# Second mixer's products taken from activations without the row's factor, which is applied at eviction

## The chip, the core and the metric

The kernel is one program on one core of a Trainium2 chip. Its engines run side by side and meet at semaphores: TensorE (PE in the profile; PEld is its weight load), VectorE (DVE), ScalarE (ACT), GpSimd (POOL), and the queues that issue DMAs (SP for most of them). The metric is the device time of one execution, in microseconds. The measured time of three executions before the change is 765.91 us (median; 765.34 to 765.93).

## What is computed

The reference runs two transformer blocks over 256 tokens of 1024 features. The first is a latent attention mixer with a mixture of experts. The second starts from the first one's normalised output, normalises again, and feeds a mixer with two halves: a gated half (strips `u` and `v_a` through GELU, layer norm, a mix over positions) and an attention half (`q`, `k`, `v` and one forget gate per head).

```python
def rms_norm(x, g):
    xf = x.astype(jnp.float32)
    y = xf * lax.rsqrt(jnp.mean(xf * xf, axis=-1, keepdims=True) + EPS)
    return (y * g.astype(jnp.float32)).astype(x.dtype)
...
    return rmsnorm(x, final_norm_g)
...
        h = rms_norm(x, norm_mix_g[l])
        z = h @ w_in[l]
        o = 0
        u_a = jax.nn.gelu(z[..., o:o + D_A], approximate=False); o += D_A
        v_a = jax.nn.gelu(z[..., o:o + D_A], approximate=False); o += D_A
...
        f_logit = z[..., o:o + N_HEADS_B] + f_bias[l].astype(z.dtype)
        out_a = spatial_gating(u_a, v_a, sg_ln_g[l], sg_w[l], sg_b[l])
        out_b = forgetting_attention(q_b, k_b, v_b, f_logit)
        x = x + jnp.concatenate([out_a, out_b], axis=-1) @ w_out[l]
```

The line `return rmsnorm(x, final_norm_g)` ends the first block; the lines behind it are the second. `q_b`, `k_b` and `v_b` are cut from `z` like the two strips. Both norms multiply a token's row by one number, so both together are a gain per feature (the product of the two gains) times one factor per token.

## The kernel before

Activations lie with features on the partitions: `xT` is 8 tiles of 128 features by 256 tokens, T is 256, KD is 8. Every float32 product that matters is split: a weight `w` is rounded to `w_hi`, its rest is `w_lo`, and the same is done to the activation (`h2_hi`, `h2_lo`); TensorE then adds three products, hi by hi, lo by hi, hi by lo. ScalarE makes the high parts (`chunk_to_hi`, one instruction for 128x1024 elements of weights), VectorE the low parts (`chunk_to_lo`). The second mixer's input weights come as five loads of 2 MB into `ring`, cut into chunks: chunks 0 to 3 are the strips `va`, 4 to 7 the strips `u`, 8 to 11 the tiles q0, k0, q1, k1, 12 to 15 `v`, 16 to 19 q2, k2, q3, k3. `w_hi` and `w_lo` have room for four chunks each, so chunk c waits until chunk c-4 has been read (`chunk2_free`).

Every engine has one queue, and its order is the order in which its part of the source is written; nothing is scheduled by a program. What a wait holds up is therefore everything that is written after it for that engine.

The stretch that the change touches begins when the last expert is done. VectorE adds the expert sum to `xT` (eight instructions, L2446). Then comes a chain: ScalarE squares the eight tiles (L981), TensorE sums them over features (L1539) and turns the sums to one number per token (L1543), VectorE, ScalarE and VectorE make reciprocal roots (L2454 to L2457; `rs` columns 2 and 3 hold the factor of both norms for the two halves of the tokens), TensorE spreads them over the partitions (L1551, banks 6 and 7), VectorE multiplies (`mix_norm`, L2462), ScalarE rounds (L988), VectorE takes the rest (`mix_low`). While TensorE has nothing to do it runs matmuls on zeros (`stay_awake`, L1251). Then it runs the strips of `va` (L1731 to L1739; for each k-tile it uses both token halves), `u` in two strips (L1221 to L1225), the eight matmuls of the forget gates (L1805, weights `wr`), tiles q0, k0, q1 (L1195), the running sums of the gates (L1777, L1771), their spreading (L1793), and k1.

`PROD2` names the products and which engine evicts them from PSUM: A for ScalarE, D for VectorE. `BANK2` gives each one its bank. From the gates hangs a chain of its own: `forget` and `forget_end` (VectorE, with exponential and logarithm on ScalarE between), row sums (PE L1777), their copy (DVE L2535), spreading, the copies `nck` (ACT L1001), eight additions of a mask on GpSimd (L719, L724), and only then the first row maximum of the attention (DVE L2225).

The attention runs 16 units (one head and one half of the queries each). For each, TensorE makes scores (L1346), VectorE adds gates and mask and takes the maximum (L2225, L2227), ScalarE the exponential (L880), VectorE the division by the sum (L2235), TensorE the transpose (L1355), ScalarE its copy (L888). Between them stand the products of `v`, q2, k2, q3, k3 and their chunks. After it come the output product, a norm, and the feed-forward part, in which TensorE runs without a gap from about 571 us to 747 us.

## Time and profile before

| | us |
|---|---|
| median of three executions | 765.91 |
| the profiled execution | 766.22 |
| its span, first to last instruction | 764.43 |
| PE busy in the span | 738.8 |
| DVE busy | 408.4 |
| ACT busy | 309.5 |
| POOL busy | 30.1 |

The profile is of one execution, which lies 0.31 us above the median. Rows of the timeline begin with the start in microseconds from the span's start, and then the busy time; a later row of an engine may begin before the busy time of an earlier one ends, since instructions overlap a little, so the pace of a row of instructions is taken from their starts. What stands in brackets is the time for which the engine was idle just before, and what ended that. One float32 matmul of 256 columns or less is recorded as two instructions.

### The profile page before, as it was taken

Reading aid. Unit: us, or ns where it says so; the run is one execution under the profiler, and the core shown is the slowest. Engines: PE = TensorE matmul, PEld = TensorE weight load, DVE = VectorE, ACT = ScalarE, POOL = GpSimd, SP = SyncE. Lnnn points to the kernel's source line nnn. Section 1 sums busy time; section 2 is a strip of 40 time slices with the busy share of each in tenths; the row PEclk is TensorE's granted clock in tenths of the full one; section 3 lists DMA queues with packets and bytes.
Section 4 is the critical chain, followed back from the end, with each engine's and each line's share of the span. In section 5 each row is a group of like instructions: output and inputs, shape, how many; then the busy total and the mean of one; then the engine's idle time right before and its main releaser. Section 6 shows DMA issues by size and latency. Waiting matters only on the chain.

```text
span 764.4 us, 11513 instructions
## 1 busy us (share of the span) xinstructions
PE 738.8 (97%) x4546; PEld 519.1 (68%) x4550; DVE 408.4 (53%) x735; ACT 309.5 (40%) x555; POOL 30.1 (4%) x42
## 2 busy tenths in 40 slices
PE   8999999999998999999999999999999999999997
PEld 3597786454696344443454346877889999999885
DVE  1594704568756122211221137877768888888443
ACT  3463202555725002001110136665656666666333
POOL 0000020033000000000000000030000000000000
PEclk9999999999999999999999999999999999999999
DMA  9973123889689899999999997305305455495101
GB/s 374 397 326 118 22 88 111 291 325 377 274 336 386 316 431 426 426 412 428 427 430 420 420 427 301 111 1 214 145 1 192 157 202 204 141 422 208 69 0 56
DMA packets 19675, 199.00 MB, mean 260 GB/s; under 512 B 2192, under 2 KB 2704, under 8 KB 4016
## 3 DMA queue, kind: packets, MB, share of 16 engines
q1 hardware_dynamic: 18720, 194.82, 63.6%
q0 software_dynamic: 624, 3.28, 1.1%
q8 instruction: 30, 0.49, 0.3%
q10 hardware_dynamic: 288, 0.30, 0.1%
q14 instruction: 13, 0.11, 0.0%
HBM read 197.34 MB, written 1.05 MB: 260 GB/s over the span
## 4 chain that ended last, share of the span: by engine, by line
PE 79%; DMA 9%; DVE 5%; ACT 4%; issue 1%; POOL 1%; SPq 0%; ACTq 0%; DVEq 0%; POOLq 0%
PE banks L1645 12%; PE banks L1959 8%; PE banks L1195 7%; PE banks L1682 6%; DMA ring<-in_w_up 5%; PE banks L1921 5%; PE banks L1919 5%; PE banks L1915 5%; PE banks L1406 2%; PE banks L1600 2%; DMA ring<-in_w_mod 2%; PE banks L1153 2%; PE banks L1443 2%; DVE w_lo L2008 2%; PE banks L1444 2%; PE banks L1445 2%
## 5 line engine op out<-in xcount | busy, mean ns | idle before, releaser
L2008 DVE TENSOR_TENSOR w_lo<-ring,w_hi 128x1024 fp32r<-128x1024 f32 (+1 forms) x122 | 145.8, 1203 | 75.9 <-ACT w_hi L1069 25.3
L1645 PE MATMUL banks<-ring,att 128*64 128x512 f32 x448 | 113.3, 593 | 2.7 <-DMA ring<-in_w_up 2.7
L1645 PEld LDWEIGHTS banks<-ring,att 128*64 128x64 f32 x448 | 39.4, 137 | 58.0 <-issue 49.9
L769 ACT ACTIVATE w_hi<-ring 128x1024 fp32r<-128x1024 f32 x50 | 52.1, 1056 | 37.8 <-PE banks L1195 22.9
L2403 DVE TENSOR_TENSOR front<-front,banks 128x512 f32<-128x512 f32 x8 | 5.5, 688 | 95.4 <-PE banks L1645 95.4
L1064 ACT ACTIVATE w_hi<-ring 128x1024 fp32r<-128x1024 f32 x44 | 46.1, 1055 | 15.9 <-PE banks L1921 8.1
L1915 PE MATMUL banks<-h_hi,w_hi 128*128 128x256 f32 x320 | 44.9, 283 | 0.0
L1919 PE MATMUL banks<-h_hi,w_lo 128*128 128x256 f32 x320 | 44.9, 283 | 0.0
L1921 PE MATMUL banks<-h_lo,w_hi 128*128 128x256 f32 x320 | 44.9, 283 | 0.0
L1915 PEld LDWEIGHTS banks<-h_hi,w_hi 128*128 128x128 f32 x320 | 41.3, 192 | 0.0
L1919 PEld LDWEIGHTS banks<-h_hi,w_lo 128*128 128x128 f32 x320 | 41.3, 192 | 0.0
L1921 PEld LDWEIGHTS banks<-h_lo,w_hi 128*128 128x128 f32 x320 | 41.3, 192 | 0.0
L2376 DVE SCALAR_TENSOR_TENSOR ysb_lo<-banks,slot_w,ysb_hi 128x512 fp32r<-128x512 f32 x16 | 12.0, 751 | 52.2 <-ACT ysb_hi L962 28.9
L962 ACT ACTIVATE ysb_hi<-banks,slot_w 128x512 fp32r<-128x512 f32 x8 | 5.5, 688 | 75.1 <-PE banks L1682 75.1
L1069 ACT ACTIVATE w_hi<-ring 128x1024 fp32r<-128x1024 f32 x22 | 23.2, 1060 | 26.9 <-PE banks L1959 25.9
L1682 PE MATMUL banks<-ring,front 128*64 128x512 f32 x128 | 29.2, 598 | 0.0
L1682 PE MATMUL banks<-big,front 128*64 128x512 f32 x64 | 28.3, 595 | 0.6 <-DVE front L2405 0.6
L2182 DVE TENSOR_REDUCE nmax<-banks 128x2 f32<-128x1024 f32 x16 | 19.6, 1224 | 12.2 <-PE banks L1406 11.9
L1959 PE MATMUL banks<-w_lo,hid_hi 128*128 128x512 f32 x88 | 25.6, 390 | 0.1
L1959 PE MATMUL banks<-w_hi,hid_hi 128*128 128x512 f32 x88 | 25.5, 389 | 0.0
L1959 PE MATMUL banks<-w_hi,hid_lo 128*128 128x512 f32 x88 | 25.5, 389 | 0.0
L858 ACT ACTIVATE osb<-banks 128x512 f32<-128x512 f32 x32 | 17.4, 600 | 19.7 <-PE banks L1415 19.7
(381 smaller groups left out, 1479.7 us busy)
## 6 DMA issues: line engine op xcount, KB each, us to landing
ring<-in_w_up SPq DMA_DIRECT2D x21, 2048.0 KB, 9.8
ring<-in_w_mod SPq DMA_DIRECT2D x11, 2048.0 KB, 9.2
ring<-in_w_down SPq DMA_DIRECT2D x9, 2048.0 KB, 12.8
ring<-in_w_in SPq DMA_DIRECT2D x8, 2048.0 KB, 18.6
ring<-in_w_gate SPq DMA_DIRECT2D x8, 2048.0 KB, 14.7
ring<-in_w_up SPq DMA_DIRECT2D x12, 1024.0 KB, 7.8
ring<-in_w_down SPq DMA_DIRECT2D x9, 1024.0 KB, 13.2
big<-in_w_down SPq DMA_DIRECT2D x8, 1024.0 KB, 14.2
```

Of the source, the lines that this page charges most:

```text
L769: nc.scalar.activation(chunk_part(w_hi, chunk, c), chunk_src(chunk, c), ACT.Copy).then_inc(chunk_hi[stage], 1)
L1064: nc.scalar.activation(granule(w_hi, j, half), up_half_of(j, half), ACT.Copy).then_inc(wide_hi, 1)
L1069: nc.scalar.activation(w_hi[:, d % 2, half, :], down_half_of(d, half), ACT.Copy).then_inc(wide_hi, 1)
L1195: last = nc.tensor.matmul(dst, chunk_part(part, chunk, c)[:, k, :], x[:, k, :], start=(part is w_hi and x is x_hi and k == 0), stop=(n == ...
L1645: last = nc.tensor.matmul(bank[2 + j][CAP * e:CAP * (e + 1), :], xs[:, k, at:at + CAP], gate_or_up(n + e, k, odd), start=(k == (4 if turne ...
L1682: last = nc.tensor.matmul(bank[2 + half][CAP * e:CAP * (e + 1), :], hidT[:, f, CAP * e:CAP * (e + 1)], w_e, start=(f == 0), stop=(f == 3))
L1915: nc.tensor.matmul(dst, granule(w_hi, j, g)[:, k, :], h2_hi[:, k, :], start=(k == 0), stop=False)
L1919: nc.tensor.matmul(dst, granule(w_lo, j, g)[:, k, :], h2_hi[:, k, :], start=False, stop=False)
L1921: last = nc.tensor.matmul(dst, granule(w_hi, j, g)[:, k, :], h2_lo[:, k, :], start=False, stop=(k == KD - 1))
L1959: return nc.tensor.matmul(ytok(q, half)[:, :], x[:, kt, q * P:(q + 1) * P], part[:, kt // 2 % 2, kt % 2, half * 512:(half + 1) * 512], sta ...
L2008: return V.tensor_tensor(dst, src, high.bitcast(F32), ALU.subtract)
L2182: V.tensor_reduce(nmax[:, u:u + 2], both[:, :, :], AX, ALU.max, negate=True).then_inc(A["maxed"], 1)
```

## The change

The mixer's products are taken from `xT` times the gain per feature (`g_both`), without the factor per token.

- ScalarE no longer waits for the norm to make `h2_hi`: `scaled_to_hi` multiplies a tile of `xT` by its gains and rounds. VectorE's `scaled_to_lo` gives the rest. Residual additions, weight chunks 0 to 3 and these steps are interleaved. The squares stand between them, and the table load for the square root behind the last of them.
- TensorE starts with `strips_of_va`. The sums of the norm stand behind these strips, then the gates' eight matmuls (from `xT` with weights `wr_x`, that VectorE has scaled by the gains), then the turn to one number per token, the first quarter of strip u0, the spreading, and the rest of u0. All `stay_awake` matmuls of this place are gone.
- The factor is applied at eviction: on ScalarE as the scale of the GELU and of `v` (one number per partition), on VectorE for q and k (`out_by_token`, one instruction with the factors spread in `by_token`) and for the gates in `forget`. So q0, k0, q1, k1, q2, k2, q3 and k3 are evicted by VectorE, where ScalarE did it.
- VectorE's order around `forget` is other: the last multiplication of the layer norm (`layer_norm_weight`) and chunk 10 now stand behind the first steps of the gates.

```diff
-PROD2 = ([("va", i, "A") for i in range(2)] + [("u", i, "A") for i in range(2)] + [("q", 0, "A"), ("f", 0, "D"),
-         ("k", 0, "A"), ("q", 1, "A"), ("rows", 0, "D"), ("cq", 0, "D")] + [("nck", i, "A") for i in range(4)] + [("k", 1, "A")]
-         + [("v", i, "A") for i in range(2)] + [(kind, i, "A") for i in range(2, 4) for kind in ("q", "k")])
+PROD2 = ([("va", i, "A") for i in range(2)] + [("u", i, "A") for i in range(2)] + [("q", 0, "D"), ("f", 0, "D"),
+         ("k", 0, "D"), ("q", 1, "D"), ("rows", 0, "D"), ("cq", 0, "D")] + [("nck", i, "A") for i in range(4)] + [("k", 1, "D")]
+         + [("v", i, "A") for i in range(2)] + [(kind, i, "D") for i in range(2, 4) for kind in ("q", "k")])
...
-        NORM_BANK = [7, 7, 0, 7]
+        NORM_BANK = [7, 7, 5, 7]
...
-            prefetch(ACT.Sqrt)
-            act.wait_ge(used, windows * 96)
-            for k in range(KD):
-                act.wait_ge(resid_m, k + 1)
-                nc.scalar.activation(sq[:, k, :], xT[:, k, :], ACT.Square).then_inc(squared, 1)
-            chunk_to_hi(1, CHUNK2, 0)
+            act.wait_ge(used, windows * 96)
+            def scaled_to_hi(ks):
+                for k in ks:
+                    act.wait_ge(resid_m, k + 1)
+                    nc.scalar.activation(h2_hi[:, k, :], xT[:, k, :], ACT.Identity, scale=g_both[:, k:k + 1]
+                                         ).then_inc(h2_hi_done, 1)
...
+            chunk_to_hi(1, CHUNK2, 0)
+            scaled_to_hi(range(4))
+            chunk_to_hi(1, CHUNK2, 1)
+            square(range(4))
+            chunk_to_hi(1, CHUNK2, 2)
+            scaled_to_hi(range(4, 6))
+            chunk_to_hi(1, CHUNK2, 3)
+            scaled_to_hi(range(6, KD))
+            square(range(4, KD))
+            prefetch(ACT.Sqrt)
             act.wait_ge(var, NORM_STEP[2] + 1)
             nc.scalar.activation(rs[:, 0:4], rs[:, 0:4], ACT.Sqrt).then_inc(std, 1)
...
-                    ins = nc.scalar.activation(vg[:, i, :], src[:, :], ACT.Gelu)
+                    ins = nc.scalar.activation(vg[:, i, :], src[:, :], ACT.Gelu, scale=rs[:, 2 + i:3 + i])
...
             prefetch(ACT.Gelu)
+            act.wait_ge(inv2, 1)
...
-            norm_sum(2, lambda: stay_awake(4, 2))
-            stay_awake(4, 2)
...
             strips_of_va()
-            product2("u", 0)
+            norm_sum(2, lambda: product2("u", 0, (0,)), gates_of_heads)
+            product2("u", 0, (1, 2, 3))
             product2("u", 1)
...
+            residual(range(4))
+            chunk_to_lo(1, CHUNK2, 0)
+            scaled_to_lo((0, 1))
+            chunk_to_lo(1, CHUNK2, 1)
+            scaled_to_lo((2, 3))
+            residual((4, 5))
+            chunk_to_lo(1, CHUNK2, 2)
+            scaled_to_lo((4, 5))
+            residual((6, 7))
+            chunk_to_lo(1, CHUNK2, 3)
+            scaled_to_lo((6, 7))
...
-            chunk_to_lo(1, CHUNK2, 0)
+            chunk_to_lo(1, CHUNK2, 4)
+            by_token = rstd[:, T:2 * T]
             dve.wait_ge(spread, 1)
+            link(V.tensor_copy(by_token, bank[6][:, 0:T]))
+            for c in range(5, 8):
+                chunk_to_lo(1, CHUNK2, c)
+            def out_by_token(kind, i):
+                n = at2(kind, i)
+                dve.wait_ge(prod2_ready, n + 1)
+                dst, scale = (q2, HD ** -0.5) if kind == "q" else (k2, 1.0)
+                V.scalar_tensor_tensor(dst[:, i, :], bank[BANK2[n]][:, 0:T], scale, by_token, ALU.mult, ALU.mult
+                                       ).then_inc(prod2_d, 1)
...
             layer_norm_end()
+            out_by_token("q", 0)
+            forget()
             chunk_to_lo(1, CHUNK2, 10)
-            forget()
+            layer_norm_weight()
+            forget_end()
+            out_by_token("k", 0)
             chunk_to_lo(1, CHUNK2, 11)
-            forget_end()
+            out_by_token("q", 1)
...
             def beside_attention(s):
+                evicted = {6: ("q", 2), 7: ("k", 2), 10: ("q", 3), 11: ("k", 3)}
                 split = {3: 16, 4: 17, 5: 18, 6: 19, 7: OUT2, 8: OUT2 + 1, 11: OUT2 + 2, 12: OUT2 + 3}
+                if s in evicted:
+                    out_by_token(*evicted[s])
```

The order on TensorE at the norm of the second mixer, before: `att` holds the squares, `cs` the zeros, `rs` the factors; line numbers are those of the kernel before.

```order
L1539 MATMUL banks0<-att,g_sq 32x256 x8
L1543 MATMUL banks0<-con,front 128x2 x2
L1251 MATMUL banks1<-cs 128x512 x4
L1551 MATMUL banks3<-con,rs 128x128 x4
L1251 MATMUL banks1<-cs 128x512 x4
L1731 MATMUL banks0<-w_hi,h2_hi 128x512 x2
L1735 MATMUL banks0<-w_lo,h2_hi 128x512 x2
L1739 MATMUL banks0<-w_hi,h2_lo 128x512 x2
```

The same place in the changed kernel, from the last step of the strips of `va` on; line numbers are the changed kernel's, and `xT,front` is the product of the gates.

```order
L1733 MATMUL banks0<-w_hi,h2_hi 128x512 x2
L1737 MATMUL banks0<-w_lo,h2_hi 128x512 x2
L1741 MATMUL banks0<-w_hi,h2_lo 128x512 x2
L1542 MATMUL banks2<-att,g_sq 32x256 x8
L1806 MATMUL banks2<-xT,front 32x256 x8
L1547 MATMUL banks2<-con,front 128x2 x2
L1224 MATMUL banks1<-w_hi,h2_hi 128x512
L1226 MATMUL banks1<-w_lo,h2_hi 128x512
L1228 MATMUL banks1<-w_hi,h2_lo 128x512
```

The sums stood ahead of all strips and stand behind the strips of `va`; between the turn (L1547) and the spreading (L1555) there are now the first six matmuls of u0 in place of the zeros.

The order on ScalarE from the last eviction of the expert part, before:

```order
L903 ACTIVATE tiny<-tiny 128x1
L978 REGISTER_ALU
L981 ACTIVATE att<-xT 128x256 x8
L769 ACTIVATE w_hi<-ring 128x1024
L984 ACTIVATE rs<-rs 128x4
```

And in the changed kernel (L982 is `scaled_to_hi`, L987 the squares, L1000 the square root, L769 a weight chunk):

```order
L982 ACTIVATE h2_hi<-xT,g_both 128x256 x2
L987 ACTIVATE att<-xT 128x256 x4
L903 ACT_TABLE_LOAD
L903 ACTIVATE tiny<-tiny 128x1
L1000 ACTIVATE rs<-rs 128x4
L769 ACTIVATE w_hi<-ring 128x1024 x2
```

Chunks 0 to 3 now stand ahead of the square root, and chunks 4 and 5 are the two behind it.

The order on VectorE in the attention at the units 6 and 7, before (L2225 and L2227 make the maximum, L2235 divides, L2008 is a weight chunk):

```order
L2225 SCALAR_TENSOR_TENSOR banks0<-banks0,small,arena 128x256
L2227 TENSOR_REDUCE nmax<-banks0 128x1
L2234 RECIPROCAL rinv<-rsum 128x1
L2235 TENSOR_SCALAR att<-att,rinv 128x256
L2008 TENSOR_TENSOR w_lo<-ring,w_hi 128x1024
L2243 CAST hid_lo<-banks2 128x256
```

And in the changed kernel, where L2495 is `out_by_token`:

```order
L2231 SCALAR_TENSOR_TENSOR banks0<-banks0,small,arena 128x256
L2233 TENSOR_REDUCE nmax<-banks0 128x1
L2240 RECIPROCAL rinv<-rsum 128x1
L2241 TENSOR_SCALAR att<-att,rinv 128x256
L2495 SCALAR_TENSOR_TENSOR arena<-banks3,front 128x256
L2014 TENSOR_TENSOR w_lo<-ring,w_hi 128x1024
L2249 CAST hid_lo<-banks2 128x256
```

One instruction stands between the division and the weight chunk; there are four such places (q2, k2, q3, k3).

## Rows read from the trace of the kernel before

**Rows 1.** Timeline of TensorE at the norm: start, busy us, instruction [idle, releaser].

```profile
454.81 3.06 PE L1539 MATMUL banks<-att,g_sq 128*32 128x256 f32 x16
458.39 0.61 PE L1543 MATMUL banks<-con,front 128*128 128x2 f32 x4 [0.52 <-DVE front L2452]
...
459.89 1.16 PE L1551 MATMUL banks<-con,rs 128*128 128x128 f32 x8
...
461.93 0.70 PE L1731 MATMUL banks<-w_hi,h_hi 128*128 128x512 f32 x2
```

**Rows 2.** Timeline of VectorE, from the last expert to the factor.

```profile
453.53 3.22 DVE L2446 SCALAR_TENSOR_TENSOR xT<-banks,mod,xT 128x256 f32<-128x256 f32 x8
...
459.03 0.16 DVE L2454 TENSOR_SCALAR rs<-banks 128x2 f32<-128x2 f32 x1 [0.70 <-PE banks L1543]
...
459.66 0.18 DVE L2457 RECIPROCAL rs<-rs 128x4 f32<-128x4 f32 x1 [0.27 <-ACT rs L984]
```

**Rows 3.** Timelines of ScalarE, VectorE and TensorE, strips of u to q0.

```profile
475.34 2.00 ACT L769 ACTIVATE w_hi<-ring 128x1024 fp32r<-128x1024 f32 x2
```

```profile
476.43 2.36 DVE L2008 TENSOR_TENSOR w_lo<-ring,w_hi 128x1024 fp32r<-128x1024 f32 x2 [2.03 <-ACT w_hi L769]
```

```profile
477.80 0.47 PE L1221 MATMUL banks<-w_hi,h_hi 128*128 128x512 f32 x1 [1.33 <-DVE w_lo L2008]
...
486.14 1.07 PE L1805 MATMUL banks<-big,wr 128*32 128x256 f32 x16
487.14 1.22 PE L1195 MATMUL banks<-h_hi,w_hi 128*128 128x256 f32 x8
```

**Rows 4.** Load landing: microseconds from issue at 432.41 us to landing.

```profile
ring<-in_w_in SPq DMA_DIRECT2D x1, 2048.0 KB, 20.8
```

**Rows 5.** Instructions by line (ns min/median/max), and timeline of L2527.

```profile
L2066 DVE SCALAR_TENSOR_TENSOR hT_lo<-arena,mod,hT_hi x16: 476/480/481, 23.2 to 55.6; 128x256 fp32r<-128x256 f32 x16
```

```profile
486.30 3.21 DVE L2527 SCALAR_TENSOR_TENSOR xT<-xT,vec,banks 128x256 f32<-128x256 f32 x8
```

**Rows 6.** Timelines of the chain from the gates to the attention, four engines.

```profile
496.29 0.18 DVE L2495 TENSOR_TENSOR small<-small 128x16 f32<-128x16 f32 x1 [0.47 <-ACT small L1036]
497.51 0.42 DVE L2535 COPY front<-banks 128x256 f32<-128x256 f32 x1 [1.04 <-PE banks L1780]
```

```profile
496.61 0.62 PE L1777 MATMUL banks<-con,small 128*8 128x256 f32 x8
```

```profile
503.31 2.82 POOL L719 TENSOR_TENSOR arena<-arena,con 128x256 f32<-128x256 f32 x4 [37.08 <-ACT arena L1001]
```

```profile
511.08 0.36 DVE L2225 SCALAR_TENSOR_TENSOR banks<-banks,small,arena 128x128 f32<-128x128 f32 x1 [1.39 <-POOL arena L724]
```

**Rows 7.** GpSimd's second four additions by line (ns min/median/max).

```profile
L724 POOL TENSOR_TENSOR arena<-arena,con x4: 727/1222/1720, 506.2 to 510.3; 128x256 f32<-128x256 f32 x4
```

**Rows 8.** Attention: busy by engine (PE PEld DVE ACT POOL, clock), then timelines.

```profile
524.00:542.00 18.00, 16.35 (x130) 13.45 (x128) 15.80 (x40) 9.98 (x30) 0.00 (x0) 1.00 0.87 350
```

```profile
528.79 0.49 PE L1346 MATMUL banks<-arena 64*128 64x128 f32 x4 [0.27 <-ACT arena L1008]
...
531.35 0.44 PE L1355 MATMUL banks<-con,att 128*128 128x128 f32 x2 [0.75 <-DVE att L2235]
```

```profile
534.37 0.49 DVE L2225 SCALAR_TENSOR_TENSOR banks<-banks,small,arena 128x256 f32<-128x256 f32 x1 [0.94 <-PE banks L1346]
```

```profile
540.30 0.44 PE L1355 MATMUL banks<-con,att 128*128 128x128 f32 x2 [0.63 <-DVE att L2235]
```

**Rows 9.** Clock: last matmul, two stretches (PEclk is third from the end), L1251.

```profile
758.82 0.39 PE L1959 MATMUL banks<-w_hi,hid_lo 128*128 128x512 f32 x1
```

```profile
760.40:761.40 1.00, 0.00 (x0) 0.00 (x0) 0.92 (x2) 0.72 (x1) 0.00 (x0) 1.00 0.00 0
761.60:762.40 0.80, 0.00 (x0) 0.00 (x0) 0.00 (x0) 0.00 (x0) 0.00 (x0) 0.50 0.26 97
```

```profile
L1251 PE MATMUL banks<-cs x59: 376/382/634, 1.4 to 461.5; 128*128 128x512 bf16 x59
```

More of the change, by code:

```diff
@@ L976, in _, with square @@
                 expert_pair(NPAIR // 2 - 1, 1, False)
-            prefetch(ACT.Sqrt)
-            act.wait_ge(used, windows * 96)
-            for k in range(KD):
-                act.wait_ge(resid_m, k + 1)
-                nc.scalar.activation(sq[:, k, :], xT[:, k, :], ACT.Square).then_inc(squared, 1)
-            chunk_to_hi(1, CHUNK2, 0)
+            act.wait_ge(used, windows * 96)
[4 more added lines that the diff above has]
+                                         ).then_inc(h2_hi_done, 1)
+            def square(ks):
+                for k in ks:
+                    nc.scalar.activation(sq[:, k, :], xT[:, k, :], ACT.Square).then_inc(squared, 1)
+            chunk_to_hi(1, CHUNK2, 0)
[7 more added lines that the diff above has]
+            square(range(4, KD))
+            prefetch(ACT.Sqrt)
             act.wait_ge(var, NORM_STEP[2] + 1)
             nc.scalar.activation(rs[:, 0:4], rs[:, 0:4], ACT.Sqrt).then_inc(std, 1)
-            chunk_to_hi(1, CHUNK2, 1)
-            for k in range(KD):
-                act.wait_ge(normed, NORMED[2] + k + 1)
-                nc.scalar.activation(h2_hi[:, k, :], h2[:, k, :], ACT.Copy).then_inc(h2_hi_done, 1)
-                if k in (2, 4):
-                    chunk_to_hi(1, CHUNK2, 1 + k // 2)
             def out_of_psum2(n):
@@ L1003, in out_of_psum2 @@
                 elif kind == "v":
-                    ins = nc.scalar.activation(v2[:, i, :], src[:, :], ACT.Copy)
-                elif kind == "q":
-                    ins = nc.scalar.activation(q2[:, i, :], src[:, 0:T], ACT.Copy, scale=HD ** -0.5)
-                elif kind == "k":
-                    ins = nc.scalar.activation(k2[:, i, :], src[:, 0:T], ACT.Copy)
+                    ins = nc.scalar.activation(v2[:, i, :], src[:, :], ACT.Identity, scale=rs[:, 2 + i:3 + i])
                 ins.then_inc(prod2_a, 1)
@@ L1540, in norm_sum @@
                 last.then_inc(sumsq, 1)
+                beside_copy()
                 pe.wait_ge(sums_copied, r - 1)
@@ L1797, in spread_rows, with gates_of_heads @@
                             last.then_inc(prod2_ready, 1)
+            def gates_of_heads():
+                pe.wait_ge(wr_scaled, 2)
+                for k in range(KD):
+                    g = 32 * (k % 4)
+                    last = nc.tensor.matmul(bank[4][g:g + 32, 0:T], wr_x[:, k, :], xT[:, k, :], start=(k < 4), stop=(k >= 4))
+                last.then_inc(f_part, 1)
             strips_of_va()
-            product2("u", 0)
+            norm_sum(2, lambda: product2("u", 0, (0,)), gates_of_heads)
+            product2("u", 0, (1, 2, 3))
             product2("u", 1)
-            pe.wait_ge(in_pool, 48)
-            for k in range(KD):
-                g = 32 * (k % 4)
-                last = nc.tensor.matmul(bank[4][g:g + 32, 0:T], wr[:, k, :], h2[:, k, :], start=(k < 4), stop=(k >= 4))
-            last.then_inc(f_part, 1)
             product2("q", 0)
@@ L2484, in forget @@
                 dve.wait_ge(prod2_ready, n + 1)
-                V.tensor_tensor(f2.rearrange("p (q h) -> p q h", q=NT),
-                                bank[BANK2[n]][:, 0:16].rearrange("p (q h) -> p q h", q=NT),
-                                bc(row[:, ROW["f_bias"]:ROW["f_bias"] + 8], 1, [P, NT, 8]), ALU.add
-                                ).then_inc(prod2_d, 1)
-                dve.wait_ge(prod2_d, 1)
+                for q in range(NT):
+                    ins = V.scalar_tensor_tensor(f2[:, 8 * q:8 * q + 8], bank[BANK2[n]][:, 8 * q:8 * q + 8],
+                                                 rs[:, 2 + q:3 + q], row[:, ROW["f_bias"]:ROW["f_bias"] + 8],
+                                                 ALU.mult, ALU.add)
+                ins.then_inc(prod2_d, 1)
+                dve.wait_ge(prod2_d, copied(PROD2, n)[1])
                 V.scalar_tensor_tensor(fa, f2, -1.0, f2, ALU.mult, ALU.min).then_inc(f_abs, 1)
@@ L2525, in _ @@
             dve.wait_ge(spread, 2)
+            dve.wait_ge(f_part, 1)
             for k in range(KD):
@@ L2554, in _ @@
                          mix_hi[1][:, 2 * b:2 * b + 2, :]).then_inc(sg_d, 1)
+            out_by_token("k", 1)
             chunk_to_lo(1, CHUNK2, 14)
```

61 lines of the change are left out of this document (26 added, 35 removed).

## The prediction

> **What bounds the kernel now.** I read the granted clock first: 2.4 GHz in every stretch with matmuls. Then the chain of work that ended last, from 450 us on. It has three parts. From 454.8 to 461.9 us it is the norm [rows 1]: sums, roots, spreading, 7.1 us in which TensorE does nothing for the products but wait and run zeros. From 462 to 571 us it changes hands: strips and tiles on TensorE, weight chunks on ScalarE and VectorE, the gates' chain, eight additions on GpSimd, then VectorE's steps in the attention [rows 6, 8]. From 571 us on it is TensorE alone without a gap, so what is won or lost before 571 us reaches the end one to one. The question is what of the 7.1 us arrives there.
>
> **The start of the strips.** The first load of the mixer's weights was issued at 432.41 us and took 20.8 us [rows 4], so it is there at 453.2 us, and the others follow before they are wanted. ScalarE makes chunk 0 by 454.2 us and then the first tiles of `h2_hi`. I give it 0.40 us for such a tile, as VectorE takes for one with a factor [rows 5]. VectorE adds four residuals from 453.53 us on at 3.22/8 = 0.40 us each [rows 2], until 455.1 us, and takes a weight chunk at about 1.2 us [rows 3]: chunk 0's low part is there at 456.3 us. TensorE ran its sums at 454.81 us before [rows 1] and now starts the strips there; its first two matmuls go at once, the next wait for 456.3 us. VectorE needs 8 x 0.40 for residuals, 4 x 1.14 for chunks and 8 x 0.40 for low parts (0.48 us busy [rows 5]): it is done at 464.5 us and stays ahead of TensorE.
>
> A 512-column matmul goes at 0.23 us: 36 of them fill the time from 477.80 to 486.14 us [rows 3]. The strips of `va` are 48, of which 46 are left at 456.3 us: 10.6 us, end at **466.9 us**. Before, 48 of them from 461.93 us [rows 1] ended near 473.5. Here the change is 6.6 us ahead.
>
> **Where it goes again.** The norm now runs behind the strips, and TensorE pays for it. Sums 1.0 us and gates 1.0 us (sixteen records of that shape take 1.07 [rows 3]), the turn 0.6 us [rows 1]: 469.6 us. The gates are only moved, so 1.0 us comes back later.
>
> Then comes the step that I take for decisive. ScalarE has its square root ahead of chunks 4 and 5, and that root waits for VectorE's variance, which waits for the turn on TensorE. From the turn's result to the factor are 0.8 us (459.03 to 459.84 us [rows 2]), to the end of the root 0.6, so 470.2 us. Only then does ScalarE make chunk 4: 1.0 us. VectorE's low part: 1.2 us. TensorE, which should run the first quarter of u0, stands from 469.6 to **472.4 us**. These six matmuls take 1.4 us; half of the spreading 0.6 (eight records, 1.16 us [rows 1]), VectorE's copy of the factors 0.45 (it stands ahead of chunk 5), chunk 5's low part 1.2: TensorE stands again from 474.9 to 476.0 us. From there TensorE has work at hand: the other 42 matmuls of u at 0.23 us take 9.7 us, to 485.7 us. Before, q0 began at 487.14 us [rows 3]. **Of 6.6 us 1.4 are left.**
>
> From q0 to the row sums TensorE took 9.5 us (487.14 to 496.61 us [rows 3, 6]) with work at hand throughout; now from 485.7 to 495.2 us. VectorE is not later: its layer norm begins when chunk 7 is done, at 478.3 us, where the low parts of before end at about 478.7 (two from 476.43 us on [rows 3]). After it chunks 8 and 9 and the eight scalings of `xT` follow as before, then q0's eviction (0.4 us) and the gates, now ahead of 2.4 us of other work. The gates' last step was done at 496.47 us [rows 6] and should be done near 494.3, so the row sums are bound by TensorE, not by it. Removing evictions from ScalarE here buys nothing, since it waited at this place anyway. Copy, spreading and `nck` follow; GpSimd starts 1.4 us earlier, at 501.9 us against 503.31, and VectorE's first maximum comes at **509.7 us** against 511.08 [rows 6].
>
> GpSimd's additions took 727 ns at best and 1720 ns at worst in the second four [rows 7]; the long ones lie beside VectorE's chunks 14 and 15. That overlap stays, so I keep its 7.7 us. The new eviction of k1 stands there too. The Trainium skill, page "GPSIMD Engine Reference", section "1. Specifications", says that GpSimd contends with VectorE instructions that have two SBUF inputs or run in a two-port mode. The eviction has one SBUF input and one in PSUM, so by that rule it costs GpSimd nothing, and the sum stands; were it priced like a chunk, four tenths of one, GpSimd would lose some 0.4 us.
>
> **The attention.** Here VectorE gets four evictions (q2, k2, q3, k3), each 128x256 from PSUM with two operands: eight of that form take 3.21 us [rows 5], 0.40 each, 1.6 us in all. VectorE is busy for 15.8 of 18 us between 524 and 542 us, more tightly bound than the page's average of 53% tells [rows 8]. And TensorE waits for it there: 0.75 us at 531.35 and 0.63 us at 540.30 us, both for a division, which stand behind q2 and k2 and behind q3 and k3 [rows 8]. Each pair is 0.8 us ahead of such a division. Upper bound 1.6 us. Lower bound zero: if VectorE's idle 0.94 us at 534.37 [rows 8] took the first pair. It does not, because VectorE waits there for scores that TensorE makes after the wait at 531.35. What comes off is small: ScalarE's chunks, for which VectorE waits at times, are earlier by the evictions that ScalarE no longer makes; a quarter of a us for that is my estimate. I take **1.35 us** lost. ScalarE's gain of 4 x 0.3 us hides behind its waits, except that k2 was a wait of 0.27 us for the scores at 528.79 us [rows 8], which VectorE now ends about 0.3 us later, inside the first 0.8.
>
> **The sum.** Profiled execution 766.22 us (span 764.43), -1.4 to the attention, +1.35 in it: 766.2 us. The median lies 0.31 lower. Forecast: **765.9 us**, no difference that can be measured. A change is told from none at about 0.2%, 1.53 us: faster means below 764.38, slower above 767.44 us. Errors of 0.5 us each in the wait for chunk 4, in the pace of VectorE and in the attention make this case's own range 765.0 to 766.9 us.
>
> **Rivals.**
>
> *The evictions are free.* The attention loses nothing, the 1.4 us arrive, and the 0.27 us at 528.79 us, a wait for ScalarE's eviction [rows 8], go too: 764.2 us. For it: ScalarE is lighter by the same instructions. Against it: the two waits of TensorE for VectorE [rows 8]. Were chunk 4 also some tenths earlier than I have it, 763.8.
>
> *The clock falls (the slower side).* `stay_awake` is gone and TensorE stands 2.8 us from 469.6 us and 1.1 us from 474.9 us, with 2.0 us of work between. At the end of the span the last matmul starts at 758.82 us, the granted clock is still full in 760.40 to 761.40 and half, 1.2 GHz, from 761.60 on, 2.4 us after the last matmul's end [rows 9]. So a wait of this length can bring it down. Price: at the lower level the same L1251 matmul took 634 ns, against 382 [rows 9], 0.25 us more; for a 512-column float32 matmul some 0.2 us. Six matmuls and half the spreading on the path: +1.8 us, 767.7. If it lasts through the next six or twelve: +3, 768.9. It decides from the point at which the wait is long enough to fell the clock; below it costs nothing. The Trainium skill, page "TensorE: Matmul & The Clock Gate", section "What's actually happening", has the throttled state as the default that activity releases, so missing activity is what would bring it back: the end of the trace agrees. Against: no stretch of the program's inside shows it, though no wait there is as long.
>
> *VectorE is later than I have it,* because it now carries residuals, low parts and evictions: chunks 4 to 7 or the layer norm slip, the 1.4 us vanish, and the attention's 1.35 stay: 767.3 us.
>
> *The change does not start early*: if the first load or chunk 0 came late, the strips would begin later than 456.3 us. Each us of it would come straight off the 1.4. The landing at 453.2 us [rows 4] speaks against it; I count it with the case before.
>
> **How the numbers follow.** Forecast 0.49 (765.0 to 766.9). Evictions free 0.25 (763.8 to 765.0), of which 0.20 below 764.38. Clock 0.17 (767.4 to 768.9). VectorE late 0.09 (766.9 to 767.9), half of it above 767.44. With some tenths from the forecast's edges: faster 0.21, same 0.56, slower 0.23. The range leaves out the outer half of the clock's case and a tail of the free one: 764.1 to 768.2 us.
>
> **What would show it.** In the changed profile: the strips' second pair at 456.3 us and their end near 467; TensorE idle 2.8 us before u0 with VectorE's chunk as releaser, and 1.1 us once more; q0 near 485.7; GpSimd near 501.9; the first maximum near 509.7; in the attention waits of TensorE for the division of about 1.5 and 1.2 us in place of 0.75 and 0.63; the feed-forward part starting within 0.5 us of 571. A granted clock under 1.00 near 472 us would be the clock's case. Wrong would be: no wait at u0, since then more than 4 us arrive at q0, or waits in the attention that have not grown.

## The result, and the profile after

The changed kernel takes 767.82 us (median of ten executions, 766.66 to 769.27) beside 765.71 us for the kernel before on the same chip (ten executions, one of them of 1050.19 us; the median of the other nine is 765.52 us). The ratio, taken without that one, is 1.0029, with a 95% interval of 1.0018 to 1.0040: slower by 1.4 to 3.1 us. The forecast was 765.9 us and no difference. The time lies inside the range, the sign is that of the rival to which the prediction gave 0.17, the falling clock.

The profiled execution took 766.77 us, span 765.0 us. It reached the norm earlier than the one of before by an amount that has nothing to do with the change: the last expert's matmul that waits for `ysb_lo` starts at 453.67 us in the trace of before and at 452.92 us in this one. All distances below are therefore taken from that matmul, called S. Its two rows, of before and of after (start, busy us, instruction [idle, releaser]):

```profile
453.67 0.38 PE L1586 MATMUL banks<-place,ysb_hi 128*128 128x256 f32 x1 [0.43 <-DVE ysb_lo L2376]
```

```profile
452.92 0.38 PE L1590 MATMUL banks<-place,ysb_hi 128*128 128x256 f32 x1 [0.43 <-DVE ysb_lo L2382]
```

TensorE from the strips of `va` to q0 in the changed kernel, which answers to [rows 1, 3]. L1733 to L1741 are the strips, L1542 the sums, L1806 the gates, L1547 the turn, L1224 products of u, L1555 the spreading, L1198 q0:

```profile
454.14 0.70 PE L1733 MATMUL banks<-w_hi,h_hi 128*128 128x512 f32 x2
455.62 0.73 PE L1737 MATMUL banks<-w_lo,h_hi 128*128 128x512 f32 x2 [0.78 <-DVE w_lo L2014]
...
466.25 1.07 PE L1542 MATMUL banks<-att,g_sq 128*32 128x256 f32 x16
467.14 1.05 PE L1806 MATMUL banks<-xT,front 128*32 128x256 f32 x16
468.11 0.61 PE L1547 MATMUL banks<-con,front 128*128 128x2 f32 x4
...
471.70 0.47 PE L1224 MATMUL banks<-w_hi,h_hi 128*128 128x512 f32 x1 [2.98 <-DVE w_lo L2014]
...
472.46 0.58 PE L1224 MATMUL banks<-w_hi,h_hi 128*128 128x512 f32 x1
...
473.70 1.91 PE L1555 MATMUL banks<-con,rs 128*128 128x128 f32 x8
...
476.62 0.47 PE L1224 MATMUL banks<-w_hi,h_hi 128*128 128x512 f32 x1 [1.01 <-DVE w_lo L2014]
...
486.24 1.11 PE L1198 MATMUL banks<-h_hi,w_hi 128*128 128x256 f32 x8
```

The strips do start early. But TensorE stands 2.98 us before the first product of u, and what runs then is slow: the spreading takes 1.91 us for eight records against 1.16 [rows 1]. The busy times by stretch say why. Columns are the stretch, its length, PE, PEld, DVE, ACT and POOL busy, the granted clock (third from the end), DMA share and GB/s:

```profile
471.00:472.00 1.00, 0.30 (x1) 0.30 (x2) 0.55 (x1) 0.98 (x2) 0.00 (x0) 1.00 0.41 172
472.00:475.00 3.00, 3.00 (x13) 2.63 (x12) 0.21 (x1) 2.99 (x6) 0.00 (x0) 0.59 0.01 5
475.00:476.00 1.00, 0.61 (x3) 0.31 (x2) 0.96 (x2) 0.80 (x1) 0.00 (x0) 0.54 0.00 0
476.00:477.00 1.00, 0.38 (x2) 0.37 (x3) 1.00 (x2) 0.00 (x0) 0.00 (x0) 1.00 0.00 0
```

The clock goes from 2.4 to 1.2 GHz shortly after work resumes: the first three products of u are still fast, the fourth, at 472.46 us, is the first slow one. It is back by 476 us. Who held TensorE: ScalarE's and VectorE's rows, which answer to [rows 2, 3] (L1000 is the square root, L769 chunks 4 and 5, L2480 and L2483 the variance and the reciprocal, L2014 the low part of chunk 4):

```profile
469.14 0.20 ACT L1000 ACTIVATE rs<-rs 128x4 f32<-128x4 f32 x1 [4.06 <-DVE rs L2481]
469.26 1.99 ACT L769 ACTIVATE w_hi<-ring 128x1024 fp32r<-128x1024 f32 x2
```

```profile
468.76 0.16 DVE L2480 TENSOR_SCALAR rs<-banks 128x2 f32<-128x2 f32 x1 [0.95 <-PE banks L1547]
...
469.38 0.18 DVE L2483 RECIPROCAL rs<-rs 128x4 f32<-128x4 f32 x1 [0.27 <-ACT rs L1000]
470.33 1.23 DVE L2014 TENSOR_TENSOR w_lo<-ring,w_hi 128x1024 fp32r<-128x1024 f32 x1 [0.77 <-ACT w_hi L769]
```

ScalarE idled 4.06 us ahead of the root, and its next two chunks, which stand behind the root in its queue, waited as long. GpSimd and the first maximum, which answer to [rows 6, 7]:

```profile
502.65 2.80 POOL L719 TENSOR_TENSOR arena<-arena,con 128x256 f32<-128x256 f32 x4 [36.97 <-ACT arena L1011]
505.54 4.83 POOL L724 TENSOR_TENSOR arena<-arena,con 128x256 f32<-128x256 f32 x4
```

```profile
510.48 0.36 DVE L2231 SCALAR_TENSOR_TENSOR banks<-banks,small,arena 128x128 f32<-128x128 f32 x1 [1.39 <-POOL arena L724]
```

And the attention, which answers to [rows 8]: first the busy times, then TensorE's waits.

```profile
524.00:542.00 18.00, 15.15 (x124) 12.92 (x122) 16.50 (x42) 8.82 (x25) 0.00 (x0) 1.00 0.86 350
```

```profile
528.43 0.49 PE L1349 MATMUL banks<-arena 64*128 64x128 f32 x4 [0.52 <-DVE arena L2495]
...
531.41 0.44 PE L1358 MATMUL banks<-con,att 128*128 128x128 f32 x2 [1.17 <-DVE att L2241]
...
540.85 0.44 PE L1358 MATMUL banks<-con,att 128*128 128x128 f32 x2 [1.16 <-DVE att L2241]
```

The three waits were 0.27, 0.75 and 0.63 us [rows 8]: 1.20 us more in all, while VectorE's busy time in the stretch rose from 15.80 to 16.50 us.

Cut at four marks (S; the start of q0; the first maximum, which waits for GpSimd; the last matmul), the span falls into pieces. Those behind S hardly vary where nothing was changed and the clock stays up; S itself varies by 1.1 us between executions, though no experiment's edit lies ahead of it, and why is not known. Each number is the difference of two starts in the trace of that kernel. The experiments below are in the table too:

| kernel | S | S to q0 | q0 to first maximum | to last matmul | to end of span |
|---|---|---|---|---|---|
| before | 453.67 | 33.47 | 23.94 | 247.74 | 5.6 |
| after | 452.92 | 33.32 | 24.24 | 248.90 | 5.6 |
| after, look1 | 453.86 | 35.88 | 24.23 | 248.94 | 5.6 |
| after, look2 | 452.97 | 33.88 | 24.23 | 248.88 | 5.6 |
| after, e8_again | 453.41 | 33.70 | 24.24 | 248.91 | 5.6 |
| e7_second | 452.80 | 33.92 | 24.24 | 248.96 | 5.6 |
| e1_zeros | 453.83 | 32.36 | 24.24 | 248.91 | 5.6 |
| e2_chunks | 452.88 | 29.70 | 24.23 | 248.89 | 5.6 |
| e5_place | 452.82 | 29.76 | 24.24 | 248.55 | 5.6 |
| e6_u_ahead | 452.88 | 27.61 | 24.24 | 248.56 | 5.6 |
| e3_evict | 453.07 | 33.49 | 23.93 | 248.89 | 5.6 |
| e4_nozeros | 452.91 | 33.48 | 23.94 | 247.73 | 5.6 |

So in its profiled execution the change gains 0.15 us up to q0, loses 0.30 up to the first maximum and 1.16 behind it: 1.3 us slower. The 0.30 us is one new wait of TensorE for a weight chunk of VectorE (chunk 10, the tile q1), which now stands behind q0's eviction and the gates:

```profile
493.85 1.22 PE L1198 MATMUL banks<-h_hi,w_lo 128*128 128x256 f32 x8 [0.30 <-DVE w_lo L2014]
```

In another execution (look1) 2.6 us more are lost between S and q0, and S comes 0.9 us later.

### The profile page after: what moved, and what is told of

It reads as the page before. It is cut to its first block, busy times and chain, and to the rows that moved or that the text cites. A ratio compares the mean times of both kernels' runs of the same rounds, so it can differ in the third digit from the quotient of the medians.

```text
span 765.0 us, 11500 instructions
## 1 busy us (share of the span) xinstructions
PE 735.4 (96%) x4542; PEld 519.5 (68%) x4542; DVE 408.9 (53%) x738; ACT 307.0 (40%) x547; POOL 30.1 (4%) x42
## 4 chain that ended last, share of the span: by engine, by line
PE 80%; DMA 10%; DVE 5%; ACT 3%; POOL 1%; issue 1%; SPq 0%; DVEq 0%; ACTq 0%; POOLq 0%
PE banks L1649 12%; PE banks L1965 8%; PE banks L1198 7%; PE banks L1686 6%; DMA ring<-in_w_up 5%; PE banks L1927 5%; PE banks L1925 5%; PE banks L1921 5%; PE banks L1409 2%; PE banks L1604 2%; DMA ring<-in_w_mod 2%; PE banks L1156 2%; PE banks L1446 2%; PE banks L1447 2%; PE banks L1448 2%; PE banks L1224 2%
## 5 line engine op out<-in xcount | busy, mean ns | idle before, releaser
L2014 DVE TENSOR_TENSOR w_lo<-ring,w_hi 128x1024 fp32r<-128x1024 f32 (+1 forms) x122 | 145.5, 1201 | 72.3 <-ACT w_hi L1072 25.3
L769 ACT ACTIVATE w_hi<-ring 128x1024 fp32r<-128x1024 f32 x50 | 51.8, 1053 | 36.7 <-PE banks L1198 22.9
```

The costliest lines, as they stand in the source:

```text
L769: nc.scalar.activation(chunk_part(w_hi, chunk, c), chunk_src(chunk, c), ACT.Copy).then_inc(chunk_hi[stage], 1)
L2014: return V.tensor_tensor(dst, src, high.bitcast(F32), ALU.subtract)
```

## The experiments

The theory: three effects of sizes known from the trace. The early start is worth about 1.1 us at q0, the four evictions cost about 1.2 us in the attention, so these two nearly cancel, and the measured loss is the clock, which falls at the 2.98 us gap. Rivals: the gap costs its idle time only and the loss lies in VectorE's load; or the attention is slower for another reason than the evictions.

### e1_zeros: the gap filled, nothing else

```diff
-            norm_sum(2, lambda: product2("u", 0, (0,)), gates_of_heads)
+            def zeros_then_u():
+                stay_awake(12, 2)
+                product2("u", 0, (0,))
+
+            norm_sum(2, zeros_then_u, gates_of_heads)
```

> The changed kernel with twelve matmuls on zeros between the turn (L1547) and the first quarter of u0, where TensorE stood idle for 2.98 us in its trace and where the granted clock then fell to 1.2 GHz for some 3.4 us. Theory A (the missing activity fells the clock, and how long it stays down differs between executions): the granted clock stays at 1.00 around 472 us, TensorE's first six matmuls of u0 take 1.4 us again and the eight spreading records 1.16 us, q0 begins about 1 us earlier, the times of the executions lie close together, and the median is 765.9 to 766.5 us against the changed kernel's 767.82. Theory B (the clock is an accident, the loss lies in the attention and in the order of ScalarE): nothing changes, 767.8 us, with the same spread.

Measured: 766.12 us (765.08 to 766.73, 12 executions), ratio to before 1.0001 (0.9991 to 1.0011). TensorE, the zeros being L1254 (twelve in the kernel, eleven in the trace), and the clock of the stretch:

```profile
469.71 2.57 PE L1254 MATMUL banks<-cs 128*128 128x512 bf16 x11
472.62 0.47 PE L1224 MATMUL banks<-w_hi,h_hi 128*128 128x512 f32 x1 [0.34 <-DVE w_lo L2018]
...
476.54 0.47 PE L1224 MATMUL banks<-w_hi,h_hi 128*128 128x512 f32 x1 [1.42 <-DVE w_lo L2018]
```

```profile
472.00:475.00 3.00, 2.66 (x16) 2.09 (x14) 0.76 (x2) 2.97 (x6) 0.00 (x0) 1.00 0.12 49
```

The first product of u starts 18.79 us behind S, against 18.78 in the changed kernel: it waits for VectorE as it did, and only the clock stays at 2.4 GHz. That alone brings the kernel back to the time of before, within what the interval leaves, -0.7 to +0.8 us (the two medians, 766.12 and 765.47, lie 0.65 us apart). So all of the measured loss but a few tenths is the clock's. In the table, q0 comes 32.36 us behind S against 33.32, 33.70, 33.88 and 35.88 us in four profiled executions of the changed kernel: the fall costs 0.96, 1.34, 1.52 and 3.52 us. This kernel is also the one that the prediction's sum describes.

### e2_chunks: the cause of the gap removed

```diff
+            for c in range(4, 6):
+                act.wait_ge(*chunk2_free(c))
+                chunk_to_hi(1, CHUNK2, c)
...
-            for c in range(4, 6):
-                split2(c)
...
+            chunk_to_lo(1, CHUNK2, 4)
...
-            chunk_to_lo(1, CHUNK2, 4)
```

ScalarE's chunks 4 and 5 go ahead of the wait for the variance, VectorE's low part of chunk 4 ahead of the copy of the sums.

> The changed kernel with ScalarE's chunks 4 and 5 and VectorE's low part of chunk 4 ahead of the square root's and the variance's waits. Theory A': the wait of 2.98 us before u0 comes from the place of these chunks in ScalarE's queue: it goes, the clock stays up with it, q0 begins 3.5 to 4.3 us earlier than in the changed kernel (near 482 us), GpSimd starts 3 to 4 us earlier, and the time is 762 to 763.5 us. Rival: VectorE, not TensorE, is what paces this stretch (it has more to do than before); then the wait moves to the chunks 5 to 7 or to the layer norm, and the gain is under 1.5 us: 765.5 to 766.5 us.

Measured: 763.47 us (763.11 to 763.86, 8 executions), ratio 0.9972 (0.9962 to 0.9982). The first product of u follows the turn without a wait, the clock is full throughout, and q0 comes 29.70 us behind S. That is 3.62 us earlier than in the changed kernel, as theory A' had it, and 2.66 us earlier than in e1_zeros, which has the full clock too: most of the length of the gap. The second wait is left, for the low part of chunk 5, which stands behind the copy of the factors, and a short one for chunk 6 is new:

```profile
472.50 0.47 PE L1225 MATMUL banks<-w_hi,h_hi 128*128 128x512 f32 x1 [1.42 <-DVE w_lo L2015]
...
474.34 0.47 PE L1225 MATMUL banks<-w_hi,h_hi 128*128 128x512 f32 x1 [0.21 <-DVE w_lo L2015]
```

### e3_evict: only the four evictions, in the kernel before

```diff
-          + [("v", i, "A") for i in range(2)] + [(kind, i, "A") for i in range(2, 4) for kind in ("q", "k")])
+          + [("v", i, "A") for i in range(2)] + [(kind, i, "D") for i in range(2, 4) for kind in ("q", "k")])
...
-                evicted = {2: ("v", 0), 4: ("v", 1), 6: ("q", 2), 7: ("k", 2), 10: ("q", 3), 11: ("k", 3)}
+                evicted = {2: ("v", 0), 4: ("v", 1)}
...
+                evicted = {6: ("q", 2), 7: ("k", 2), 10: ("q", 3), 11: ("k", 3)}
+                if s in evicted:
+                    kind, i = evicted[s]
+                    n = at2(kind, i)
+                    dve.wait_ge(prod2_ready, n + 1)
+                    V.tensor_scalar((q2 if kind == "q" else k2)[:, i, :], bank[BANK2[n]][:, 0:T],
+                                    HD ** -0.5 if kind == "q" else 1.0, None, ALU.mult).then_inc(prod2_d, 1)
```

> The kernel before, in which only the evictions of q2, k2, q3 and k3 are moved from ScalarE to VectorE. Theory A: VectorE is the bound there; TensorE's two waits for its division grow from 0.75 and 0.63 us to about 1.2 each, and the time is 1.0 to 1.3 us above the kernel before (766.8 us). Rival: moved evictions hide in waits: within 0.3 us of the kernel before.

Measured: 766.96 us (766.07 to 769.14, 12 executions), ratio 1.0021 (1.0012 to 1.0029).

```profile
528.41 0.49 PE L1346 MATMUL banks<-arena 64*128 64x128 f32 x4 [0.51 <-DVE arena L2566]
531.38 0.44 PE L1355 MATMUL banks<-con,att 128*128 128x128 f32 x2 [1.16 <-DVE att L2236]
540.84 0.44 PE L1355 MATMUL banks<-con,att 128*128 128x128 f32 x2 [1.17 <-DVE att L2236]
```

The three waits are those of the changed kernel, with the releasers in the same places. The piece behind the first maximum is 248.89 us, against 247.74 before and 248.90 in the changed kernel, and the pieces ahead of it are those of before. So the whole cost in the attention, 1.15 us, is the four evictions, each 0.42 us on VectorE, for which TensorE already waited at these places. Theory A holds. The ratio speaks for 0.9 to 2.2 us; the trace's figure lies in it.

### e4_nozeros: the kernel before without the zeros around its norm

```diff
-            norm_sum(2, lambda: stay_awake(4, 2))
-            stay_awake(4, 2)
+            norm_sum(2)
```

> The kernel before, without the zeros around the norm of the second mixer (twelve matmuls recorded at L1251). Theory A (a short lack of activity fells the clock, depending on the execution): TensorE is idle for 0.9 and 1.1 us, with 0.5 to 1 us of matmuls between; in part of the executions the clock falls to 1.2 GHz and the median rises by 0.5 to 2 us with a wider spread. Theory B (only a wait of over 2 us fells it): no difference from the kernel before, 765.7 us.

Measured: 766.57 us (765.55 to 768.38, 12 executions), ratio 1.0014 (1.0005 to 1.0022). TensorE's new gaps, and the clock:

```profile
459.12 1.16 PE L1551 MATMUL banks<-con,rs 128*128 128x128 f32 x8 [0.89 <-DVE rs L2456]
...
461.17 1.19 PE L1730 MATMUL banks<-w_hi,h_hi 128*128 128x512 f32 x2 [0.88 <-ACT h_hi L988]
```

```profile
458.50:461.30 2.80, 1.29 (x9) 1.13 (x9) 2.44 (x6) 1.85 (x4) 0.00 (x0) 0.94 1.02 424
461.30:464.70 3.40, 3.40 (x9) 2.68 (x10) 3.03 (x7) 1.77 (x4) 0.00 (x0) 0.55 1.03 435
464.70:466.00 1.30, 1.30 (x8) 1.05 (x7) 1.30 (x3) 0.01 (x1) 0.53 (x1) 1.00 0.86 366
```

Two gaps of 0.9 us with 1.2 us of work between them are enough to let the clock fall, in the second of them, for some 3.4 us. Ahead of them lie a wait of 0.52 us and the sums, whose sixteen records take 3.05 us here, because they come at the pace of the squares, against 1.07 us in the changed kernel, so TensorE was sparsely used for longer than the two gaps. No single wait here is over 0.9 us: theory B, a wait of over 2 us, falls, and theory A holds. In this execution, the fastest of the twelve, it costs nothing at q0 (33.48 us behind S, 33.47 before): the wait for chunk 5 of [rows 3], 1.33 us, shrinks to 0.53 us and swallows it. Over all executions the kernel is a little slower, by 0.4 to 1.7 us. Which of them pay, and where, no trace shows.

### e5_place: two evictions moved into idle time

```diff
-                evicted = {6: ("q", 2), 7: ("k", 2), 10: ("q", 3), 11: ("k", 3)}
+                evicted = {5: ("q", 2), 7: ("k", 2), 9: ("q", 3), 11: ("k", 3)}
...
-                if s in evicted:
+                if s in evicted and s != 5:
...
+                if s == 5:
+                    out_by_token(*evicted[s])
```

Made on e2_chunks. In unit 5 the eviction stands behind the weight chunk.

> This is e2_chunks (763.47 us) with two of the four evictions that the change gave to VectorE moved one unit of the attention earlier: the second query chunk directly behind the weights of its unit, and the fourth likewise, where VectorE otherwise stood idle waiting for scores (0.65 and 0.94 us). Theory A: the evictions cost what they do because they stand between a score and its softmax at the places where TensorE then waits 1.16 us; moved into idle time, those waits fall back towards 0.75 and 0.63 us and the time falls 0.6 to 0.8 us, to about 762.7. Theory B: VectorE is the pace of these units whatever the order, the 0.42 us evictions only move the wait, and the time stays at 763.5 (763.2 to 763.8).

Measured: 762.93 us (761.94 to 765.66, 8 executions), ratio 0.9963 (0.9949 to 0.9978).

```profile
524.42 0.49 PE L1350 MATMUL banks<-arena 64*128 64x128 f32 x4 [0.18 <-DVE arena L2496]
527.39 0.44 PE L1359 MATMUL banks<-con,att 128*128 128x128 f32 x2 [1.16 <-DVE att L2242]
536.84 0.44 PE L1359 MATMUL banks<-con,att 128*128 128x128 f32 x2 [1.16 <-DVE att L2242]
```

Half of theory A: the wait for scores fell from 0.52 to 0.18 us, the two waits for divisions stayed at 1.16. The piece behind the first maximum is 0.34 us shorter, not 0.6 to 0.8, and that is the first wait alone. The ratios of the two kernels, 0.9972 and 0.9963, can't be told apart; the rows can.

### e6_u_ahead: the low parts threaded between the steps of the norm

```diff
-            for c in range(4, 6):
+            for c in range(4, 8):
...
-            for c in range(6, 8):
-                split2(c)
...
+            chunk_to_lo(1, CHUNK2, 5)
...
+            chunk_to_lo(1, CHUNK2, 6)
...
-            for c in range(5, 8):
-                chunk_to_lo(1, CHUNK2, c)
+            chunk_to_lo(1, CHUNK2, 7)
```

Made on e5_place. The first part is ScalarE's, the rest VectorE's: chunk 5 behind the copy of the sums, 6 behind the reciprocal, 7 behind the copy of the factors.

> This is e5_place with ScalarE's normalisation-free chunks 4 to 7 all ahead of the root, and VectorE's low halves 5, 6 and 7 each between two short steps of the norm. Theory A: the 1.42 us wait of TensorE inside the u products in e2_chunks is VectorE reaching those low halves too late, behind the norm's short steps; with them ahead there is no such wait, the first query product starts about 1.8 us earlier (near 480.7), and the time is about 1.7 us under e5_place, near 761. Theory B: what follows (row factors, then the strips scaled by them, then GpSimd's table work ahead of the first max) is paced by the norm, which these low halves now delay; then the wait moves behind the u products and the time is within 0.5 us of e5_place.

Measured: 760.68 us (760.24 to 761.21, 5 executions), ratio 0.9934 (0.9922 to 0.9947), on the same chip as e5_place: 2.25 us less.

```profile
468.57 0.48 PE L1223 MATMUL banks<-w_hi,h_hi 128*128 128x512 f32 x1
...
470.04 1.05 PE L1554 MATMUL banks<-con,rs 128*128 128x128 f32 x8
```

TensorE has no wait from the turn to q0, which comes 27.61 us behind S, 2.15 us earlier than in e5_place; the norm, delayed by a low part here and there, is late for nobody. Theory A holds. This is the fastest kernel of the study, 5.0 us under the one before.

### look1 and look2: the changed kernel twice more

> The changed kernel once more, for one look. Its ten executions lay in two groups, 766.7 to 767.2 us and 768.4 to 769.3 us. Theory A: in both the clock falls behind the 2.98 us gap before the first u product, and the slower group is a longer fall (half clock from about 472.6 to 477 or beyond) or a second one. Theory B: the slower group has its extra time elsewhere, at a wait for a transfer.

> The same look again, so that a member of each group is seen: an execution with a span near 765 shows half clock for about 2.5 us behind the gap, one with a span near 767 for 4 us or more, or twice.

Measured: 770.42 us and 767.36 us. In look1 the same gap of 2.98 us stands ahead of u, until 472.65 us; then:

```profile
471.00:472.00 1.00, 0.00 (x0) 0.00 (x0) 0.72 (x1) 1.00 (x2) 0.00 (x0) 0.98 1.00 426
472.00:475.00 3.00, 2.35 (x6) 1.90 (x7) 0.50 (x1) 2.97 (x6) 0.00 (x0) 0.50 0.20 85
...
477.00:480.00 3.00, 1.99 (x6) 1.48 (x5) 3.00 (x3) 0.00 (x0) 0.00 (x0) 0.50 0.00 0
480.00:481.00 1.00, 1.00 (x4) 0.71 (x4) 1.00 (x2) 0.00 (x0) 0.00 (x0) 0.50 0.00 0
481.00:482.00 1.00, 1.00 (x4) 0.81 (x3) 0.93 (x3) 0.00 (x0) 0.00 (x0) 0.50 1.09 246
482.00:484.00 2.00, 2.00 (x10) 1.61 (x9) 1.97 (x2) 0.00 (x0) 0.00 (x0) 0.95 0.73 279
```

Half clock for about ten microseconds instead of three and a half, from about 472 us on, ahead of the first product, and q0 35.88 us behind S. In look2 the fall is a short one, from about 471.7 us, where the first product starts at 471.78 us, to about 475.1 us, and all six products ahead of the spreading are slow:

```profile
471.00:472.00 1.00, 0.22 (x1) 0.26 (x2) 0.63 (x1) 0.98 (x2) 0.00 (x0) 0.83 0.35 147
472.00:475.00 3.00, 3.00 (x9) 2.42 (x10) 0.00 (x0) 2.99 (x6) 0.00 (x0) 0.50 0.01 5
475.00:476.00 1.00, 0.82 (x7) 0.63 (x6) 0.55 (x2) 0.88 (x1) 0.00 (x0) 0.96 0.00 0
```

The pieces behind q0 are those of the other executions, so theory A holds for what is lost between S and q0. It does not account for all of the spread: look1's span is 3.5 us longer than the profiled execution's, 2.56 us of it by the longer fall and 0.94 us ahead of S.

### e7_second and e8_again: does the second wait prolong the fall?

```diff
+            stay_awake(6, 3)
             product2("u", 0, (1, 2, 3))
```

e8_again is the changed kernel itself, on the same chip.

> The changed kernel with six zero matmuls behind the spreading, in TensorE's second wait of the place (1.01 us in the profiled execution of the changed kernel); its first wait, 2.98 us, stays bare, so the clock still falls there. What is open is why the granted clock came back at about 475.5 us in one look of the changed kernel and at about 481.9 us in another, 2.9 us later at the end. Theory A: the second wait keeps the clock down in the slow ones; with it filled, every execution has the short fall, the times lie within 0.8 us of each other and the median is near 766.9, 1 us under e8_again's. Theory B: how long the clock stays down hangs on when the fall comes and not on the second wait; then both groups, near 767 and near 769, are still there, and the median is that of e8_again within 0.5 us.

> The changed kernel itself on the same chip, so that the spread of its times can be set beside that of e7_second. As before two groups are expected, one near 767 us with a short fall of the clock and one 768.4 to 770.4 us with a long one; neither theory says which has more members.

Measured: e7_second 767.37 us (766.37 to 769.96, 11 executions), ratio 1.0031 (1.0021 to 1.0040); e8_again 768.03 us, the median of ten executions between 766.06 and 770.53 us (with an eleventh, of 4146 us, it is 768.20), ratio 1.0035 (1.0022 to 1.0048), which repeats the first result. In e7_second's profiled execution the zeros follow the spreading without a wait and the fall is a short one, to about 475.1 us. With the second wait filled the times still reach 768.7 to 770.0 us, in three of eleven executions, at mean granted clocks of 0.994. None of the three was profiled; read from their times and clocks, a long fall does not need the second wait bare: theory B for that point. Whether a filled wait makes it rarer is open: the medians differ by 0.66 us, more than B allowed, but the ratios can't be told apart. The times form no two clean groups in either kernel, so that part of the expectation fell.

## Why the prediction was wrong, point by point

**The step that failed is the sum's, where the gap of 2.8 us before u0 was priced at its idle time alone.** The prediction named the mechanism, the place and the sign that would show it, and then gave it 0.17. All it had against it was that "no stretch of the program's inside shows it", and it conceded itself that "no wait there is as long". That was no evidence: the waits inside the program before are short (the longest ahead of a matmul is 1.57 us, at 195.68 us) or filled with zeros, so its trace could not show what a longer one does, and e4_nozeros brought a fall about by taking the zeros away. The change took them away too and made a gap longer than any before; with a mechanism known to exist at the end of the span [rows 9], this should have been the likeliest case. What the runs showed in place of an idle time alone: the same gap, filled (e1_zeros), gives q0 0.96 to 3.52 us earlier. The rival's price was right in size: +1.8 us forecast for the short fall and +3 for the long one, 0.96 to 1.52 and 3.52 measured. In the profiled execution the short one is cheaper because three of the six products still run at the full clock, and because part of it hides in the second wait, which is 1.01 us there against 1.42 at full clock. That the time of 767.82 us lies inside the stated range comes from this rival, not from the forecast's sum.

**The rest of the sum held,** best read in e1_zeros, which is the forecast's own case. From S: sums forecast at 13.2 us (466.9 against S of 453.67), 13.33 measured. First wait 2.8 forecast, 2.98 measured where it is bare; second 1.1, 1.42 with the full clock; q0 32.0, 32.36. From q0 to the first maximum 24.0, 24.24: VectorE was taken to be nowhere late, and a chunk of it is, by 0.30 us. Attention +1.35, +1.17: e3_evict assigns it to the evictions alone. The forecast put all of it on the two waits for divisions, at about 1.5 and 1.2 us; they are 1.17 and 1.16 us, and the wait for scores took the rest, 0.52 against 0.27 us. Gained before q0 1.11 us, lost behind it 0.30 and 1.17: +0.36 us, where the forecast had -0.05; 0.3 us less gain and the new wait stand against 0.2 us less in the attention. The measured ratio is 1.0001. GpSimd's second four additions took 4.83 us against 4.78 before, and 4.79 us in e3_evict, which leaves k1 with ScalarE: k1's eviction from PSUM (VectorE, 505.86 us), which stands beside them, costs them 0.05 us at most, and not the 0.4 us of the other case. That agrees with the Trainium skill, page "GPSIMD Engine Reference", section "1. Specifications", which has GpSimd contend with VectorE instructions that have two SBUF inputs or run in a two-port mode.

**The rivals.** "Evictions free" is excluded by e3_evict. "VectorE late" is true by 0.3 us and no more. "Does not start early" is excluded by the strips at 454.14 and 455.62 us. The prediction also said that 6.6 us of early start dwindle to 1.4 and why: e2_chunks and e6_u_ahead give back 2.66 and another 2.15 us of it by reordering alone. So both causes that it named are shown: the square root ahead of chunk 4 for the first wait, and the copy of the factors ahead of chunk 5's low part for the second.

## What to carry to other kernels

A gap in TensorE's queue has two prices, its length and the slow matmuls behind it; where a change removes filler matmuls or opens a wait, count both, and take the absence of a fall in the old trace as evidence only if that trace has a bare gap as long. When work is pulled ahead of a chain of short steps, pull the preparation of its operands ahead in every engine's queue too: here weight chunks that stood behind a square root and behind the copy of the factors ate much of the early start of 6.6 us, and reordering gave 4.8 us of it back. An eviction moved to the engine for which another already waits costs most of its length, 1.15 of 1.7 us here.

## What the runs showed of the hardware that was not expected

- The granted clock fell in the second of two bare gaps of 0.9 us with 1.2 us of work between them and sparse work ahead (e4_nozeros), and at one of 2.98 us. Single waits of 1.42 us (e2_chunks) and 1.57 us (the kernel before), with dense or filled stretches beside them, left it at 1.00. The Trainium skill, page "TensorE: Matmul & The Clock Gate", section "What's actually happening", calls the throttled state the default that activity releases and missing activity brings back; the traces agree.
- The same gap in the same program brings a fall of about 3.4 us in some executions and about 10 us in another, and 0.96 to 3.52 us of time. The fall began from 0.7 us ahead of the first product (look1) to 0.8 us behind it (the first profiled execution). The second wait does not decide it alone (e7_second). That section of the page says that what decides on the clock does not start anew with the kernel. S varies between 452.80 and 453.86 us by execution, and look1, with the longest fall, has the latest S. That fits, but five traces with this gap are too few, so the cause stays open.
- The fall is likely and not certain. All five traces with the bare gap show it, but one execution each of the changed kernel (766.67 us), e7_second (766.37) and e8_again (766.32) has a mean granted clock of 1.000, and a fall of 3.4 us would take 0.002 off. The kernel before, with its zeros, is not free of falls either: three executions, of 767.72, 767.88 and 768.44 us, have a mean clock of 0.996, where its profiled execution has 0.998. None of the six executions named was profiled.
- A fall can be free: in e4_nozeros a wait behind it shrank by 0.80 us and q0 was not later.
